# Last batch of the gate matrix written in four pieces on two queues and awaited in the next stage

## The chip, the cores and the metric

The kernel runs on one core of one Trainium2 chip, as one program of 48136 instructions. The metric is the device time of one execution in microseconds (us). A core has a matmul engine (TensorE, PE), a vector engine (VectorE, DVE), an activation engine (ScalarE, ACT), a general engine (GpSimd, POOL) and a synchronization engine (SyncE, SP). Transfers between the core's memory and main memory are issued from an engine's instruction stream and then run on 16 DMA engines which all queues share.

## The reference

Two transformer blocks on 512 tokens of width 1024. The part around the change is the product-key expert layer (PEER) of the first block: each token scores 128 + 128 sub-keys for each of 8 heads, keeps 16 of the pairs, and sums the outputs of these experts out of 128 x 128.

```python
def peer_ffn(x, w_query, sub_keys_1, sub_keys_2, w_down, w_up):
    ...
    top_s, pos = lax.top_k(cand, PEER_TOPK)
    expert_idx = jnp.take_along_axis(cand_idx, pos, axis=-1)
    gate = jax.nn.softmax(top_s, axis=-1).astype(x.dtype)
    ...
        u = w_down[ib]
        act = jax.nn.gelu(jnp.einsum("td,thkd->thk", xb, u), approximate=False) * gb
        v = w_up[ib]
        return jnp.einsum("thk,thkd->td", act, v)
```

Its result is added to the residual; a norm, the second block (attention, gating, 32 routed experts) and the last norm follow.

## The kernel before, in words

The program is a row of stages. Each is a `Stage` with its own buffers and semaphores, and `Stage.__exit__` clears the semaphores and puts a barrier over all engines (line 66), so a stage starts when every engine has finished the one before.

PEER isn't computed by gathering for the main 384 tokens (TD): it is computed densely. `stage_gate_matrix` (lines 1379 to 1551) turns the chosen experts and their weights into a full matrix of gates: for each token, 128 x 128 numbers that are zero but for the chosen pairs. It goes through the tokens in BATCHES = 6 batches of TB = 64. PE multiplies one-hot rows (line 1444), ACT copies the products out of PSUM into `out` (line 1488), a double buffer of 2 x 32 KB on each of 128 partitions, and SP writes each finished batch to the tensor `peer_gates` in main memory (line 1545, 4096 KB, one row of 32 KB for each partition; in a row, 128 keys by 64 tokens). Batch 5, the last, lies in the second half of `out`.

In the gaps, PE also computes the hidden values of experts in advance (line 1455); ACT bends them into `stash` (line 1466) and SP saves them as `peer_early` (line 1528, 192 KB each). SP also loads ahead what the next stage needs first: the first tiles of `wd`, `wu` and `hid`. SP's last waits (lines 1549 to 1551) are for the writes of the gates, the writes of the stash and these loads.

`stage_peer_experts` (lines 1554 to 1842) then runs STEPS = 64 steps over key rows, two rows in each step. A step has 24 matmuls of 384 columns (`late`, lines 1646 to 1648: hidden values of one key row) and 36 of 512 columns (`up`, lines 1655 to 1657: outputs of two key rows, accumulated in `Y` over the whole stage). Each float32 operand is split in a high part (ACT) and a low part (DVE). DVE multiplies the hidden values by the gates `gt` (lines 1753 and 1759), which SP reads back with `load_gt` (line 1588): 768 KB for two steps, four keys of all six batches, in runs of 1 KB. The 128 tokens left over (the first 128) are done by gather on POOL (`gather`, lines 1627 and 1630: 1 MB for each of 128 pairs, rows of 8 KB) and two DVE instructions for each pair (lines 1781 and 1793). The order of work at the start, by engine:

- SP: `load_gt(0, 0)`, two tiles of `wd` (line 1611), `load_gt(1, 1)`, and then `ahead` for each step: `wd`, `hid`, `wu` and, at every second step, `gt`, each behind the wait for the buffer that it overwrites.
- POOL: up to four gathers, then one for each that DVE has used up.
- ACT: `split_wd` of the first tile, `split_wu`, then `split_hid`, which waits for DVE's first multiplication by `gt`, then `split_wd` of the second tile.
- DVE: `low_wd`, then `weigh`, which waits for `gt`, and so on.
- PE: `late(0, 0)` after the first `low_wd`; `late(1, 1)` after the second.

Of the kernel before, what the change touches and what calls it, by code (L numbers as in the profile page):

```python
# [11 lines left out]
U32 = mybir.dt.uint32  # L12
# [1366 lines left out]
def stage_gate_matrix(nc, c, a):  # L1379
# [6 lines left out]
    with Stage(nc, "gates") as s:  # L1386
# [18 lines left out]
        wd_d = a["peer_wdT"]  # L1405
        wu_d = a["peer_pairs"]
        with s.block() as block:

# [52 lines left out]
            def _(act):  # L1461
# [40 lines left out]
                for b in range(BATCHES):  # L1502
# [9 lines left out]
                    if b < BATCHES - 1:  # L1512
                        with act.Fori(1, per) as q:
                            take(b, q)
                    else:
                        for q in range(1, per):
                            take(b, q, R * (per - q))
                early(2 * BATCHES - 2)
                early(2 * BATCHES - 1)

            @block.sync
            def _(sp):
# [13 lines left out]
                for b in range(BATCHES):  # L1536
# [7 lines left out]
                    sp.wait_ge(taken, R * per * (b + 1) + R)  # L1544
                    sp.dma_start(c.gates[b], out[:, b % 2, :, :].rearrange("p i t -> p (i t)")).then_inc(saved[b % 2], 16)
                save(2 * BATCHES - 2)
                save(2 * BATCHES - 1)
                for b in range(2):
                    sp.wait_ge(saved[b], 16 * (BATCHES // 2))
                    sp.wait_ge(stashed[b], 16 * BATCHES)  # L1550
# [3 lines left out]
def stage_peer_experts(nc, c, a):  # L1554
# [5 lines left out]
    with Stage(nc, "experts") as s:  # L1560
        wd = c.hT[:].rearrange("p k t -> p (k t)").rearrange("p (j n) -> p j n", j=4)
        wu, hid = c.wu, c.hid
        wd_hi, wd_lo = (s.sb(f"wd_{n}", [P, 2, D], F32R) for n in ("hi", "lo"))
        wu_hi, wu_lo = (s.sb(f"wu_{n}", [P, 2, 2, D], F32R) for n in ("hi", "lo"))
        hid_hi, hid_lo = (s.sb(f"hid_{n}", [P, 2, TD], F32R) for n in ("hi", "lo"))
        new = s.sb("new", [P, 2, TD])
        new_hi, new_lo = (s.sb(f"new_{n}", [P, 2, TD], F32R) for n in ("hi", "lo"))
        gt = s.sb("gt", [P, 2, BATCHES, 4 * TB])
        pair = s.sb("pair", [P, 4, 2 * D])
        slot = s.sb("slot", [P, 2 * U], U32)  # L1570
        dot = s.sb("dot", [P, 2, 2])
        bent = s.sb("bent", [P, 2, 2])
        part = s.sb("part", [P, 2, 2])
        Y = s.ps("Y", [P, 6, 512])
        H = s.ps("H", [P, 2, 512])
        wd_in, hid_in, paired = ([s.sem(f"{n}{i}") for i in range(4)] for n in ("wd_in", "hid_in", "paired"))
        wu_in, gt_in = ([s.sem(f"{n}{i}") for i in range(2)] for n in ("wu_in", "gt_in"))
        (wd_h, wd_l, wu_h, wu_l, hid_h, hid_l, new_h, new_l, h_done, gelued, gated, weighed, y_done, slotted, dotted,
         pair_bent, parted, added, paced, chain) = (s.sem(n) for n in (
# [3 lines left out]
        with s.block() as block:  # L1583

            @block.sync
            def _(sp):
# [17 lines left out]
                for i in range(4):  # L1604
                    if i < 2:
                        sp.sem_inc(wd_in[i], 16)
                        sp.sem_inc(wu_in[i], 16)
                    sp.sem_inc(hid_in[i], 16)
                load_gt(0, 0)
                for i in range(2, 4):  # L1610
                    sp.dma_start(wd[:, i, :], wd_d[STEPS + i]).then_inc(wd_in[i], 16)
                load_gt(1, 1)
                with sp.Fori(0, STEPS // U - 1) as r:
                    for u in range(U):
# [5 lines left out]
            def _(pool):  # L1620
                pool.sem_inc(added, 4)

                def gather(it, r, u, e):
# [1303 lines left out]
class Common:  # L2927
# [18 lines left out]
    def peer(self, ctx):  # L2946
# [3 lines left out]
        self.pair_gate = self.sb(ctx, "pair_gate", [P, PAIRS])  # L2950
        self.early = self.nc.dram_tensor("peer_early", [STEPS, P, TD], F32, kind="Internal").ap()
        self.gates = self.nc.dram_tensor("peer_gates", [BATCHES, NK, NK * TB], F32, kind="Internal").ap()

# [104 lines left out]
```

## Time and profile before

| | |
|---|---|
| median of 3 runs | 3527.06 us (3523.44 to 3539.63) |
| the profiled execution | 3532.37 us, its span 3530.6 us |
| PE busy in the span | 3202.8 us, 91% |
| DVE, ACT, POOL busy | 76%, 51%, 22% |
| gate stage, first to last matmul | about 939 to 1099 us |
| dense expert stage | about 1112 to 1910 us |

Times in the trace are microseconds from the span's start. The page names each instruction by its line and by output and inputs; SPq is SP's instruction stream, in which the transfers are issued. In the table by stretches, the column PEclk is the TensorE clock that was granted, as a share of full speed, and the DMA share is the mean busy share of the 16 DMA engines (it can pass 1, as the records of transfers overlap).

### The profile page before, as it was taken

To read this page: it belongs to the slowest core of one execution; us is meant where nothing else is said; L and a number is where in the kernel's file an instruction comes from. 1 tells how busy PE (TensorE), PEld (TensorE's weight loads), DVE (VectorE), ACT (ScalarE), POOL (GpSimd) and SP (SyncE) were. 2 spreads that over 40 slices of the span, in tenths; PEclk is the share of its full clock that TensorE was granted. 3 is DMA by queue.
4 is the path that set the end of the run, shared out by engine and by line. 5 is a ranking of instruction groups with operands and counts; after the bars stand their busy time and mean duration, and the time that the engine had idled before them with its cause. 6 is when DMAs were issued, how large, how long until landed. Compare 5 with 4: busy or idle time off the path is not lost. (4 is left out here: it accounts for less than half of the span.)

```text
span 3530.6 us, 48136 instructions
## 1 busy us (share of the span) xinstructions
PE 3202.8 (91%) x16519; PEld 2754.8 (78%) x16519; DVE 2697.6 (76%) x3822; ACT 1807.9 (51%) x2168; POOL 762.8 (22%) x478
## 2 busy tenths in 40 slices
PE   5999777999887999999997966599999999999996
PEld 5997666999887888888886845377788888878883
DVE  5786554696496878788887354599999999999994
ACT  3343342333585333333333241377777777777783
POOL 0000001445221444454542000211111111111110
PEclk8899788999999999999998976699999999999997
DMA  4220031334456999999985111699999999999993
GB/s 128 60 78 25 1 120 66 109 124 164 152 236 255 341 351 337 348 347 346 357 327 190 73 55 40 229 346 351 352 353 363 351 359 360 363 362 359 370 354 149
DMA packets 196091, 852.19 MB, mean 241 GB/s; under 512 B 22274, under 2 KB 104978, under 8 KB 152276
## 3 DMA queue, kind: packets, MB, share of 16 engines
q1 hardware_dynamic: 167492, 699.66, 54.0%
q0 software_dynamic: 28496, 151.16, 10.6%
q8 instruction: 65, 1.06, 0.1%
q14 instruction: 38, 0.31, 0.0%
HBM read 809.19 MB, written 59.38 MB: 246 GB/s over the span
## 5 line engine op out<-in xcount | busy, mean ns | idle before, releaser
L2704 DVE TENSOR_TENSOR moe_w_lo<-all_raw,moe_w_hi 128x2048 fp32r<-128x2048 f32 x298 | 676.0, 2286 | 68.8 <-ACT moe_w_hi L2644 66.4
L2644 ACT ACTIVATE moe_w_hi<-all_raw 128x2048 fp32r<-128x2048 f32 x298 | 567.0, 1915 | 84.8 <-PE moe_GU L2610 70.6
L2610 PE MATMUL moe_GU<-moe_w_hi,moe_x_lo 128*128 128x512 f32 x1056 | 418.6, 396 | 0.0
L2609 PE MATMUL moe_GU<-moe_w_lo,moe_x_hi 128*128 128x512 f32 x1056 | 418.1, 396 | 0.0
L2608 PE MATMUL moe_GU<-moe_w_hi,moe_x_hi 128*128 128x512 f32 x1056 | 418.1, 396 | 0.0
L1153 POOL TENSOR_TENSOR score_w_lo<-all_hT,score_w_hi 128x1024 fp32r<-128x1024 f32 x68 | 167.7, 2466 | 706.8 <-ACT score_w_hi L1218 706.8
L1781 DVE SCALAR_TENSOR_TENSOR experts_pair<-experts_pair,all_x_first 128x1024 f32<-128x1024 f32 x128 | 156.5, 1223 | 130.8 <-DMA experts_pair<-in_peer_pairs,experts_slot 130.8
L1630 POOL DMA_INDIRECT experts_pair<-in_peer_pairs,experts_slot x128 | 223.5, 1746 | 114.7 <-POOL experts_slot L1627 110.1
L2609 PEld LDWEIGHTS moe_GU<-moe_w_lo,moe_x_hi 128*128 128x128 f32 x1056 | 198.9, 188 | 48.8
L2610 PEld LDWEIGHTS moe_GU<-moe_w_hi,moe_x_lo 128*128 128x128 f32 x1056 | 198.9, 188 | 47.8
L2608 PEld LDWEIGHTS moe_GU<-moe_w_hi,moe_x_hi 128*128 128x128 f32 x1056 | 199.2, 189 | 46.3
L2704 DVE TENSOR_TENSOR moe_w_lo<-all_hT,moe_w_hi 128x2048 fp32r<-128x2048 f32 x98 | 223.0, 2284 | 2.4 <-ACT moe_w_hi L2644 1.4
L1627 POOL COPY experts_slot<-all_pair_id 128x1 uint32 x128 | 151.4, 1183 | 322.3 <-DVE all_h L1793 293.0
L2618 PE MATMUL moe_Y<-moe_w_hi,moe_hid_hi 128*128 128x512 f32 x528 | 215.2, 408 | 0.7 <-DVE moe_hid_lo L2734 0.7
L2619 PE MATMUL moe_Y<-moe_w_lo,moe_hid_hi 128*128 128x512 f32 x528 | 209.2, 396 | 0.0
L2620 PE MATMUL moe_Y<-moe_w_hi,moe_hid_lo 128*128 128x512 f32 x528 | 209.1, 396 | 0.0
L2644 ACT ACTIVATE moe_w_hi<-all_hT 128x2048 fp32r<-128x2048 f32 x98 | 187.5, 1914 | 38.6 <-PE moe_GU L2610 23.2
L2552 POOL DMA_INDIRECT pair_rows<-moe_y,moe_slot x33 | 48.1, 1457 | 728.2 <-ACT moe_y L2687 728.2
L1177 PE MATMUL score_H<-all_x_hi,score_w_hi 128*128 128x384 f32 (+1 forms) x544 | 190.3, 350 | 8.6 <-DVE all_x_lo L1291 8.6
L1178 PE MATMUL score_H<-all_x_lo,score_w_hi 128*128 128x384 f32 (+1 forms) x544 | 189.7, 349 | 0.0
L1179 PE MATMUL score_H<-all_x_hi,score_w_lo 128*128 128x384 f32 (+1 forms) x544 | 189.6, 349 | 0.0
L1646 PE MATMUL experts_H<-all_x_hi,experts_wd_hi 128*128 128x384 f32 x512 | 172.7, 337 | 16.2 <-DVE experts_wd_lo L1763 16.2
(473 smaller groups left out, 8170.3 us busy)
## 6 DMA issues: line engine op xcount, KB each, us to landing
all_raw<-in_w_moe SPq DMA_DIRECT2D x149, 2048.0 KB
all_hT<-in_w_moe SPq DMA_DIRECT2D x49, 2048.0 KB, 9.4
all_hT<-in_peer_wdT SPq DMA_DIRECT2D x128, 512.0 KB
all_wu<-in_peer_pairs SPq DMA_DIRECT2D x64, 1024.0 KB, 13.5
peer_gates<-gates_out SPq DMA_DIRECT2D x6, 4096.0 KB
experts_gt<-peer_gates SPq DMA_DIRECT2D x32, 768.0 KB, 9.7
all_hT<-in_w_in SPq DMA_DIRECT2D x40, 512.0 KB
out_w<-in_w_out SPq DMA_DIRECT2D x12, 1024.0 KB
```

The lines of the kernel that those rows point to most:

```text
L1177: pe.matmul(out, left, c.x_hi[:, k, at:T], start=(k == 0), stop=False)
L1178: pe.matmul(out, left, c.x_lo[:, k, at:T], start=False, stop=False)
L1179: mm = pe.matmul(out, low, c.x_hi[:, k, at:T], start=False, stop=(k == KD - 1))
L1630: pool.indirect_dma_start(out=pair[:, v, :], out_offset=None, in_=a["peer_pairs"][:, :], in_offset=bass.IndirectOffsetOnAxis(ap=slot[:, n: ...
L2608: pe.matmul(out, x_hi[:, kx, :], hi[:, k, :], start=False, stop=False)
L2609: pe.matmul(out, x_hi[:, kx, :], lo[:, k, :], start=False, stop=False)
L2610: mm = pe.matmul(out, x_lo[:, kx, :], hi[:, k, :], start=False, stop=(kx == KD - 1))
L2618: pe.matmul(Y[:, b, :], hid_hi[:, h, :], hi[:, f, cols], start=(h == 0), stop=False)
L2619: pe.matmul(Y[:, b, :], hid_hi[:, h, :], lo[:, f, cols], start=False, stop=False)
L2620: mm = pe.matmul(Y[:, b, :], hid_lo[:, h, :], hi[:, f, cols], start=False, stop=(h == KD - 1))
L2644: act.activation(w_hi[p % RING][:], piece_of(r, p), ACT.Copy).then_inc(w_high, 1)
L2704: dve.tensor_tensor(w_lo[p % RING][:], piece_of(r, p), w_hi[p % RING][:].bitcast(F32), ALU.subtract).then_inc(w_low, 1)
```

## The change

The last batch of gates is written not as one transfer of 4096 KB but as four of 1024 KB, by key: piece 0 holds keys 0 to 31 of each row, and so on (rows of 8 KB). SP issues piece 0; ACT issues pieces 1 to 3, behind its last copy out of PSUM and ahead of its last two stash activations. The pieces have two semaphores of their own (`c.tail`), which the gate stage doesn't wait for. It still waits for the other writes of the gates, for all writes of the stash, and for the loads ahead.

In the expert stage SP waits for piece 0 ahead of `load_gt(0, 0)`, and for the other three behind `load_gt(1, 1)`, ahead of the loop of `ahead`. POOL waits for those three ahead of its first gather. The gathers' buffer `pair` now lies where batch 5 lay in `out` (bytes 49152 to 81920 of each partition); `wu_hi`, `wu_lo`, `gt` and small buffers lie below it, with an unused filler `lead` and `hid_hi`, and the other buffers above. No instruction changes its shape.

```diff
+        def piece_in(i):
+            return out[:, (BATCHES - 1) % 2, i * NK // 4:(i + 1) * NK // 4, :].rearrange("p i t -> p (i t)")
+        def piece_out(i):
+            return c.gates[BATCHES - 1][:, i * (NK // 4) * TB:(i + 1) * (NK // 4) * TB]
...
+                act.wait_ge(taken, R * per * BATCHES + R)
+                for i in range(1, 4):
+                    act.dma_start(piece_out(i), piece_in(i)).then_inc(c.tail[1], 16)
                 early(2 * BATCHES - 2)
                 early(2 * BATCHES - 1)
...
-                    sp.dma_start(c.gates[b], out[:, b % 2, :, :].rearrange("p i t -> p (i t)")).then_inc(saved[b % 2], 16)
+                    if b + 1 < BATCHES:
+                        sp.dma_start(c.gates[b], out[:, b % 2, :, :].rearrange("p i t -> p (i t)")).then_inc(saved[b % 2], 16)
+                    else:
+                        sp.dma_start(piece_out(0), piece_in(0)).then_inc(c.tail[0], 16)
                 save(2 * BATCHES - 2)
                 save(2 * BATCHES - 1)
                 for b in range(2):
-                    sp.wait_ge(saved[b], 16 * (BATCHES // 2))
+                    sp.wait_ge(saved[b], 16 * ((BATCHES - b) // 2))
                     sp.wait_ge(stashed[b], 16 * BATCHES)
...
-        wd_hi, wd_lo = (s.sb(f"wd_{n}", [P, 2, D], F32R) for n in ("hi", "lo"))
         wu_hi, wu_lo = (s.sb(f"wu_{n}", [P, 2, 2, D], F32R) for n in ("hi", "lo"))
-        hid_hi, hid_lo = (s.sb(f"hid_{n}", [P, 2, TD], F32R) for n in ("hi", "lo"))
-        new = s.sb("new", [P, 2, TD])
-        new_hi, new_lo = (s.sb(f"new_{n}", [P, 2, TD], F32R) for n in ("hi", "lo"))
         gt = s.sb("gt", [P, 2, BATCHES, 4 * TB])
-        pair = s.sb("pair", [P, 4, 2 * D])
-        slot = s.sb("slot", [P, 2 * U], U32)
         dot = s.sb("dot", [P, 2, 2])
         bent = s.sb("bent", [P, 2, 2])
         part = s.sb("part", [P, 2, 2])
+        slot = s.sb("slot", [P, 2 * U], U32)
+        lead = s.sb("lead", [P, D - 28 - 2 * TD])
+        hid_hi = s.sb("hid_hi", [P, 2, TD], F32R)
+        pair = s.sb("pair", [P, 4, 2 * D])
+        wd_hi, wd_lo = (s.sb(f"wd_{n}", [P, 2, D], F32R) for n in ("hi", "lo"))
+        hid_lo = s.sb("hid_lo", [P, 2, TD], F32R)
+        new = s.sb("new", [P, 2, TD])
+        new_hi, new_lo = (s.sb(f"new_{n}", [P, 2, TD], F32R) for n in ("hi", "lo"))
...
+        s.sems += c.tail
...
+                sp.wait_ge(c.tail[0], 16)
                 load_gt(0, 0)
                 for i in range(2, 4):
                     sp.dma_start(wd[:, i, :], wd_d[STEPS + i]).then_inc(wd_in[i], 16)
                 load_gt(1, 1)
+                sp.wait_ge(c.tail[1], 48)
...
                 pool.sem_inc(added, 4)
+                pool.wait_ge(c.tail[1], 48)
...
+        self.tail = [self.nc.alloc_semaphore(f"gate_tail{i}") for i in range(2)]
```

## Rows read from the trace of the kernel before

**Rows 1.** Busy time by stretch; columns stand in the view's own second line.

```profile
core 0: us, PE busy (x) PEld busy (x) DVE busy (x) ACT busy (x) POOL busy (x), PEclk, DMA share, GB/s
1101.00:1104.00 3.00, 0.00 (x0) 0.00 (x0) 0.00 (x0) 0.00 (x0) 0.00 (x0) 0.60 1.21 513
1104.00:1105.00 1.00, 0.00 (x0) 0.00 (x0) 0.00 (x0) 0.00 (x0) 0.00 (x0) 0.50 0.08 33
1105.00:1109.00 4.00, 0.00 (x0) 0.00 (x0) 0.00 (x0) 0.00 (x0) 0.00 (x0) 0.50 1.22 524
1109.00:1110.00 1.00, 0.00 (x0) 0.00 (x0) 0.00 (x0) 0.00 (x0) 0.00 (x0) 0.50 0.04 12
1110.00:1112.00 2.00, 0.00 (x0) 0.00 (x0) 0.00 (x0) 0.00 (x0) 0.00 (x0) 0.50 0.53 191
1112.00:1114.00 2.00, 0.00 (x0) 0.00 (x0) 0.34 (x1) 1.43 (x2) 0.18 (x1) 0.50 0.00 0
1116.00:1126.00 10.00, 9.41 (x47) 9.09 (x47) 7.13 (x10) 5.41 (x8) 4.97 (x6) 0.87 1.03 408
1150.00:1880.00 730.00, 730.00 (x3538) 644.73 (x3537) 599.20 (x830) 269.48 (x416) 353.59 (x237) 1.00 0.92 343
```

**Rows 2.** Timeline at the border of the stages: start, duration, engine, line [idle before].

```profile
1098.71 0.60 ACT L1488 ACTIVATE gates_out<-gates_ps 128x512 f32<-128x512 f32 x1 [0.99 <-PE gates_ps L1444]
1099.03 0.34 PE L1455 MATMUL gates_H<-all_x_hi,gates_wd_lo 128*128 128x384 f32 x1
1099.20 0.87 ACT L1466 ACTIVATE gates_stash<-gates_H 128x384 f32<-128x384 f32 x2
1099.33 0.33 SPq L1545 DMA_DIRECT2D peer_gates<-gates_out  x1
1099.71 1.37 SPq L1528 DMA_DIRECT2D peer_early<-gates_stash  x2
1112.57 1.06 ACT L1689 ACTIVATE experts_wd_hi<-all_hT 128x1024 fp32r<-128x1024 f32 x1 [12.51 <-SPq L1606]
...
1113.03 0.39 SPq L1588 DMA_DIRECT2D experts_gt<-peer_gates  x1
...
1114.22 1.73 POOL L1630 DMA_INDIRECT experts_pair<-in_peer_pairs,experts_slot  x1 [1.05 <-issue]
```

**Rows 3.** SP's waits around the border: us in total, times, longest.

```profile
SPq L1550 <- DMA peer_early<-gates_stash: 10.4, 1, 10.4
```

**Rows 4.** The stash's and first gates' transfers by line.

```profile
L1528 SPq DMA_DIRECT2D peer_early<-gates_stash x12: 332/343/904, 970.5 to 1100.2; - x12
...
DMA to landing us min/median/max: 5.4/6.1/11.3
```

**Rows 5.** Timeline of the expert stage's first steps on DVE.

```profile
1118.28 0.56 DVE L1753 TENSOR_TENSOR all_hid<-all_hid,experts_gt 128x384 f32<-128x384 f32 x1 [3.40 <-DMA experts_gt<-peer_gates]
...
1120.38 1.23 DVE L1763 TENSOR_TENSOR experts_wd_lo<-all_hT,experts_wd_hi 128x1024 fp32r<-128x1024 f32 x1
...
1129.12 1.22 DVE L1781 SCALAR_TENSOR_TENSOR experts_pair<-experts_pair,all_x_first 128x1024 f32<-128x1024 f32 x1
...
1134.27 0.56 DVE L1753 TENSOR_TENSOR all_hid<-all_hid,experts_gt 128x384 f32<-128x384 f32 x1 [2.31 <-DMA experts_gt<-peer_gates]
...
1142.54 1.22 DVE L1763 TENSOR_TENSOR experts_wd_lo<-all_hT,experts_wd_hi 128x1024 fp32r<-128x1024 f32 x1
```

**Rows 6.** Timeline of the expert stage's first steps on PE.

```profile
1114.94 0.69 PE L1646 MATMUL experts_H<-all_x_hi,experts_wd_hi 128*128 128x384 f32 x1 [15.57 <-DVE experts_wd_lo L1763]
...
1121.66 0.44 PE L1646 MATMUL experts_H<-all_x_hi,experts_wd_hi 128*128 128x384 f32 x1 [0.59 <-DVE experts_wd_lo L1763]
...
1146.53 0.33 PE L1646 MATMUL experts_H<-all_x_hi,experts_wd_hi 128*128 128x384 f32 x1
```

**Rows 7.** The loads of `gt`: landing after issue.

```profile
DMA to landing us min/median/max: 8.5/9.7/19.7
```

**Rows 8.** Durations in the expert stage by tile: ns min/median/max.

```profile
L1767 DVE TENSOR_TENSOR experts_wu_lo<-all_wu,experts_wu_hi x128: 1214/1221/1236, 1118.8 to 1891.1; 128x1024 fp32r<-128x1024 f32 x128
```

## The prediction

> **What bounds the kernel now.** I read the busy time by stretch first, to see which engine is never idle beside the change. From 1150 to 1880 us, nearly the whole dense expert stage, PE is busy for 730 of 730 us at the full granted clock, and the DMA engines for 0.92 of it [rows 1]. So the stage goes by PE: when it starts earlier by some time, it ends earlier by that time, as long as transfers keep up. Nothing that the change moves inside this stretch can win anything, and DMA has only 8% of air there.
>
> Then I read the timeline at the border of the two stages. The last matmul of the gate stage starts at 1099.03 and the first of the expert stage at 1114.94, with 15.57 us idle [rows 2, 6]. That gap is all that the change can reach: 15.6 us are 0.44% of the run, and no version of this edit can save more there.
>
> What fills the gap is seen in SP's waits and in the stretches. SP issues the 4096 KB write at 1099.33 and the two last stash writes up to about 1101.1 [rows 2]. It then waits 10.4 us at line 1550, the wait for the **stash**, and not at line 1549 for the gates [rows 3]: the small transfers stand behind the large one in the same queue and land last, at about 1111.5. The bytes are seen to flow from 1100 to 1104, from 1105 to 1109 and from 1110 to 1111 or so: 4.19 + 0.39 = 4.58 MB in 11.1 us, 413 GB/s with the two holes counted [rows 1]. After 1111.5 come barrier and start: ACT begins at 1112.57, `load_gt(0, 0)` is issued at 1113.03 [rows 2]. From about 1111 to 1114 the DMA engines move nothing [rows 1].
>
> Last, the start of the expert stage on DVE and PE. The first matmuls need no gates. DVE then waits 3.40 us for `gt`, which is there at 1118.28, 5.25 us after its issue [rows 2, 5]; behind that stands the low part of the second `wd` (1120.38 + 1.23 = 1121.6), and PE's second group starts with it at 1121.66 after 0.59 us idle [rows 5, 6]. So the landing of the first `gt` is on the path too: what delays it delays PE one for one. From there on PE isn't idle.
>
> **The change part by part.**
>
> Removed from the path: the wait for the large write. But the wait that SP was seen in, for the stash, stays in the gate stage. The question is when the two stash writes land now. They are issued from SP's queue behind 1 MB instead of 4 MB, while 3 MB go through ACT's queue on the same engines.
>
> Issue times: ACT's last copy ends at 1099.31 [rows 2]. Three issues come now ahead of its two stash activations. ACT issues no transfer in this trace, so their price is bounded by SP's 0.33 us and by POOL's indirect 1.73 us each [rows 2]: 1.0 to 5.2 us. I take 1.0, since these are plain transfers like SP's. The activations (0.87 us for the pair) then end at about 1101.2, and the last stash is issued at 1101.5 instead of before 1101.1. The shortest landing of such a write is 5.4 us [rows 4]: not before 1106.9.
>
> Flow: 1.44 MB go through SP's queue. If both queues get the same bytes, they are through when 2.88 MB have moved, 7.0 us at 413 GB/s, at 1107.0, and landed with the 0.4 us that the last bytes took before (1111.1 to 1111.5) at **1107.4**. If the queues take turns row by row, each DMA engine has 8 + 8 + 8 rows of SP (8 KB, then twice 1.5 KB) against 24 rows of 8 KB of ACT, and both end together, at **1111.5** as before. No two queues from SP and ACT are seen together in this trace, so I take the middle, rounded to 1109.0, and keep both ends. The border moves by 2.5 us (bounds 4.1 and 0).
>
> The Trainium skill, DMA: Bandwidth & Descriptors, section on queues, rings and completion order, says that a DMA engine alternates between queues by whole packets of some 9 to 17 descriptors. By that, an estimate from that page, the SP queue would get a share of turns near that of its transfers: 1 MB, stash, stash, each against about 1 MB of ACT's, so the last stash would be through with two or three of the three pieces, at 1108.5 to 1111. The same page's rules for kernel authors speak against any gain from the second queue as such: spreading transfers over issuing engines brings no bandwidth. The traces so far have nothing that contradicts either.
>
> Start of the next stage: SP's wait for piece 0 costs nothing, as that piece is ahead of the stash in its queue. `load_gt(0, 0)` is issued at 1113.0 - 2.5 = 1110.5; its bytes began to flow about 1 us after issue before (issue 1113.03, none moved until 1114 [rows 1, 2]), so at 1111.5, when the last piece is through (all bytes need the same 11.1 us from 1100). Delay of `gt`: 0; at the good bound (issue at 1108.9, flow from 1109.9) up to 1.2 us of shared flow.
>
> SP's wait for pieces 1 to 3 stands ahead of the loop of `ahead`, behind both `load_gt`. Queued behind it are the loads of `wd`, `hid` and `wu` for later steps. It is over at about 1111.5, before SP would get there (1110.5 + 2). POOL's wait holds back all gathers until about 1111.5, where they would start at 1114.2 - 2.5 = 1111.7: nothing. If it lasted 2 us longer, the first use of a gathered pair at 1129.12 covers it, and the next use of DVE waits for `gt` anyway, 2.31 us before 1134.27 [rows 5].
>
> What is late next: after the first steps DMA works off a backlog (408 GB/s from 1116 to 1126 [rows 1]). The tightest place is the low part of `wd` that DVE ends at 1143.8, with PE taking it at 1146.53: 2.8 us of slack [rows 5, 6]. Transfers too start 2.5 us earlier, as they move out of the dead time from 1111 to 1114, so this stays uncovered by a hair but holds.
>
> The other order of buffers: same instructions, same shapes. DVE's `wu_lo` runs over four places and all 128 lie between 1214 and 1236 ns [rows 8], so address has cost nothing so far: 0. Two more semaphores to clear, two waits, more instructions: 0.
>
> **Sum.** -2.5 (border) + 0 (gt) + 0 (all else) = -2.5 us, against the profiled execution's 3532.37 us: 3529.9. That execution is 5.3 us above the median of the runs; from the median, 3527.06 - 2.5 = **3524.6 us**.
>
> **The rivals.**
>
> A, the stash stays last (no gain, so the change does not do what it says). By the row-by-row turns above, or because ACT's three issues cost nearer 1.73 us each (stash issued at 1105.7, landed at 1111.1 or later), or because the barrier's drain on ACT waits for transfers still under way; in this trace all had landed by the time of the barrier, so it can't tell. Against it: the short landing of 5.4 us for a stash write with little ahead of it [rows 4]. Also here: rows of 8 KB may flow slower than those of 32 KB; at the stage's 343 GB/s [rows 1] 4.58 MB take 13.4 us, 2.3 us more. Time: 3526 to 3529.5, say 3527.
>
> B, slower: the first `gt` starves. It is read in runs of 1 KB and may now share the engines with rows of 8 KB of the pieces. The slowest load of `gt` landed 19.7 us after issue [rows 7], which fits the second one, issued at the stage's start beside the gathers and waited for until 1134.27 [rows 5]; the first took 5.25. If the first were held as long, PE would lose 14.5 us against at most 4.1 won: 3537.5. It decides from a delay above what the border gains (2.5 to 4.1 us). Against it: by then at most 0.6 MB of the pieces are left, 1.5 us of flow.
>
> C, the full 4.1 us, with at most 0.3 us lost to the shared flow: 3523.0.
>
> D, the new places in memory or the shifted code change the pace of a stage. One per cent of the expert stage's 790 us would be 7.9 us, either way: 3519 or 3535. Only the narrow spread of [rows 8] speaks to it, and against it.
>
> **How the numbers follow.** Forecast with its surroundings (-1 to -3.5 us) 0.42; A 0.30; C 0.13; B 0.08; D 0.07, half each way. The range: from D's good side to the middle of B and D's bad side, widened because a median of three runs of this kernel itself lies within 12 us of its highest run: 3516 to 3535. The likeliest case alone: 3522 to 3528. A change of 0.5% is 17.6 us, about what a measurement of this kernel can tell from no change; the whole gap is 15.6 us, so faster by that much needs D or a fluke, and slower needs B at its worst with D on top. Faster 0.03, within 0.94, slower 0.03.
>
> **What the profile of the changed kernel would show.** SP's wait at the end of the gate stage still ends with a stash write, near 1109 (forecast), 1111.5 (A) or 1107.4 (C) if the last copy of ACT ends at 1099.3. Three issues on ACT's queue of about 0.35 us each. The first matmul of the expert stage 2.5 us earlier after ACT's last copy than the 15.6 us of before; the first multiplication by `gt` 5 to 6 us after its load's issue (B: more than 8). The stretch from 1150 to 1880 with the same matmul count and PE never idle; any other count is D. I am wrong if the gap shrinks by more than 4.1 us, which needs a stash write that lands faster than any did before, or if PE is idle after its second group.

## The result and the profile after

| | before | changed |
|---|---|---|
| median, the two run in turns | 3529.86 us (8 runs) | 3542.93 us (8 runs, 3535.12 to 3550.39) |
| ratio | | 1.0037, 95% interval 1.0023 to 1.0052 |
| the profiled execution, its span | 3532.37, 3530.6 us | 3535.12, 3533.3 us |

The change makes the kernel slower by some 13 us. That is above the whole range of the forecast (3516 to 3535) and has the other sign than its likeliest case. The profiled execution is the fastest of the eight, so it shows only a part of the loss: its span is 2.7 us longer, though by the rows below the border and the expert stage together take 11.4 us more. The parts ahead of and behind them happened to be 8.7 us shorter in it.

**The border** did what rival A says. The changed kernel's timeline answers to [rows 2] (start, duration, engine, line, what ended the idle time before it):

```profile
1096.29 0.60 ACT L1495 ACTIVATE gates_out<-gates_ps 128x512 f32<-128x512 f32 x1 [0.99 <-PE gates_ps L1451]
1096.92 2.05 ACTq L1527 DMA_DIRECT2D peer_gates<-gates_out  x3
1099.07 0.87 ACT L1473 ACTIVATE gates_stash<-gates_H 128x384 f32<-128x384 f32 x2 [2.18 <-issue]
1110.52 1.06 ACT L1708 ACTIVATE experts_wd_hi<-all_hT 128x1024 fp32r<-128x1024 f32 x1 [10.58 <-SPq L1622]
...
1096.91 0.33 SPq L1558 DMA_DIRECT2D peer_gates<-gates_out  x1
1099.59 1.57 SPq L1538 DMA_DIRECT2D peer_early<-gates_stash  x2
1110.98 0.39 SPq L1604 DMA_DIRECT2D experts_gt<-peer_gates  x1
```

The three issues take ACT 2.05 us, and they aren't alike (count: duration in ns as min/median/max):

```profile
L1527 ACTq DMA_DIRECT2D peer_gates<-gates_out x3: 401/445/1142, 1096.9 to 1097.8; - x3
```

Two take 0.40 and 0.45 us, not far from SP's 0.33 for a lone one, and the third 1.14. From the end of ACT's last copy (1096.89) to the issue of the first `gt` pass 14.09 us; before they were 1113.03 - 1099.31 = 13.72 [rows 2]. The border has moved by 0.37 us the wrong way. SP's waits there (line, what ended them, us in total, times, longest) answer to [rows 3]:

```profile
SPq L1563 <- DMA peer_early<-gates_stash: 8.3, 1, 8.3
SPq L1538 <- ACT gates_stash L1473: 2.3, 1, 2.3
```

The wait at the end is shorter by 2.1 us only because SP comes to it later: it waits 2.3 us for ACT's stash activations first (0.4 before). It still ends with a stash write, at about 1109.5 (ACT starts 1.06 us later, as it did before). Busy time by stretch in the changed kernel (columns: us, PE, PEld, DVE, ACT and POOL busy with their counts, clock, DMA share, GB/s):

```profile
1099.00:1103.00 4.00, 0.00 (x0) 0.00 (x0) 0.00 (x0) 0.87 (x2) 0.00 (x0) 0.59 1.04 426
1103.00:1105.00 2.00, 0.00 (x0) 0.00 (x0) 0.00 (x0) 0.00 (x0) 0.00 (x0) 0.50 1.00 412
1105.00:1108.00 3.00, 0.00 (x0) 0.00 (x0) 0.00 (x0) 0.00 (x0) 0.00 (x0) 0.50 1.01 406
1108.00:1109.00 1.00, 0.00 (x0) 0.00 (x0) 0.00 (x0) 0.00 (x0) 0.00 (x0) 0.50 0.81 317
1109.00:1111.00 2.00, 0.00 (x0) 0.00 (x0) 0.00 (x0) 0.48 (x1) 0.04 (x1) 0.50 0.00 0
1150.00:1880.00 730.00, 730.00 (x3488) 635.58 (x3488) 601.30 (x820) 268.36 (x409) 251.12 (x236) 1.00 0.92 341
```

The bytes flow without a hole up to just before 1109, when the stash is through too: both queues end together, and 1109 to 1111 stay empty as 1111 to 1114 did before [rows 1]. How they share the engines shows in the packets of each queue (q1 is SP's, q10 ACT's: packets, MB, share of 16 engines), here from 1099.9 to 1100.2, from 1100.2 to 1100.5 and from 1100.5 to 1100.8 us:

```profile
q1 hardware_dynamic: 16, 0.13, 109.6%
q10 hardware_dynamic: 16, 0.13, 103.0%
q1 hardware_dynamic: 16, 0.13, 103.7%
```

Sixteen rows of 8 KB from one queue, as many as there are DMA engines, then sixteen from the other: the queues take turns row by row. From 1104 to 1108, with SP's queue at the stash's rows of 1.5 KB, the counts stay alike and the bytes don't:

```profile
q10 hardware_dynamic: 183, 1.37, 83.3%
q1 hardware_dynamic: 189, 0.27, 17.8%
```

**The expert stage** is where the time went. PE is still busy for 730 of 730 us at full clock, but it gets through 3488 matmuls, not 3538 [rows 1]. The rows of one output buffer show why (line, operands, count: duration in ns as min/median/max, first and last start in us, form). First two of the kernel before:

```profile
L1655 PE MATMUL experts_Y<-experts_wu_hi,experts_hid_hi x384: 387/389/390, 1125.9 to 1905.5; 128*128 128x512 f32 x192
L1655 PE MATMUL experts_Y<-experts_wu_hi,experts_new_hi x384: 389/389/389, 1130.1 to 1909.6; 128*128 128x512 f32 x192
```

and the same two of the changed one:

```profile
L1674 PE MATMUL experts_Y<-experts_wu_hi,experts_hid_hi x384: 392/396/399, 1123.8 to 1914.4; 128*128 128x512 f32 x192
L1674 PE MATMUL experts_Y<-experts_wu_hi,experts_new_hi x384: 392/396/399, 1128.0 to 1918.6; 128*128 128x512 f32 x192
```

The same instruction with the same shape takes 396 ns for 389, and from the first of these starts to the last are 790.6 us for 779.6: **+11.0 us**. This difference of two starts is "the stage" below.

A second execution of the changed kernel (3551.82 us, span 3550.0, above all eight of the table) has a stage of 795.5 us; experiments 3 and 16, with the same places of the buffers, have 795.6 and 795.5:

```profile
L1674 PE MATMUL experts_Y<-experts_wu_hi,experts_hid_hi x384: 389/394/398, 1127.3 to 1922.8; 128*128 128x512 f32 x192
1150.00:1880.00 730.00, 730.00 (x3467) 633.63 (x3466) 597.15 (x818) 269.16 (x409) 273.46 (x233) 1.00 0.92 341
```

Matmuls overlap, so what counts is the distance between starts. PE's timeline in the middle of the stage, before:

```profile
1499.62 0.39 PE L1655 MATMUL experts_Y<-experts_wu_hi,experts_hid_hi 128*128 128x512 f32 x1
...
1501.66 0.39 PE L1655 MATMUL experts_Y<-experts_wu_hi,experts_new_hi 128*128 128x512 f32 x1
```

and in this second execution of the changed kernel:

```profile
1499.61 0.39 PE L1675 MATMUL experts_Y<-experts_wu_lo,experts_new_hi 128*128 128x512 f32 x1
...
1501.71 0.39 PE L1675 MATMUL experts_Y<-experts_wu_lo,experts_new_hi 128*128 128x512 f32 x1
```

Nine matmuls in 2.04 and in 2.10 us: 226.7 and 233.3 ns each. Averaged over the starts from 1150 to 1880 us, the 512-column ones went from 227.8 to 233.3 ns (36 in each of 63 steps: 12.5 us; before, too, the whole stretch is a little slower than the nine shown) and the 384-column ones from 174.4 to 176.7 (24 in each: 3.5 us), together 16.0 us of the 15.9 seen. In the first execution of the changed kernel the 512-column ones start every 233.3 ns too, but the 384-column ones every 173.4, no slower than before; that is why its stage is shorter.

### The profile page after: what moved, and what is told of

The parts are those of the page before. It is cut to its first block and busy times, and to the rows that moved or that the text cites. A ratio compares the mean times of both kernels' runs of the same rounds, so it can differ in the third digit from the quotient of the medians.

```text
span 3533.3 us, 48143 instructions
## 1 busy us (share of the span) xinstructions
PE 3210.9 (91%) x16519; PEld 2753.6 (78%) x16519; DVE 2705.9 (77%) x3822; ACT 1811.4 (51%) x2168; POOL 649.5 (18%) x478
## 3 DMA queue, kind: packets, MB, share of 16 engines
q8 instruction: 65, 1.06, 0.1%
## 5 line engine op out<-in xcount | busy, mean ns | idle before, releaser
L1714 ACT ACTIVATE experts_wu_hi<-all_wu 128x1024 fp32r<-128x1024 f32 x128 | 135.5, 1059 | 214.0 <-PE experts_Y L1676 204.9
L1649 POOL DMA_INDIRECT experts_pair<-in_peer_pairs,experts_slot x128 | 180.7, 1412 | 114.6 <-POOL experts_slot L1646 110.0
L1786 DVE TENSOR_TENSOR experts_wu_lo<-all_wu,experts_wu_hi 128x1024 fp32r<-128x1024 f32 x128 | 156.7, 1224 | 57.4 <-ACT experts_wu_hi L1714 56.8
## 6 DMA issues: line engine op xcount, KB each, us to landing
peer_gates<-gates_out SPq DMA_DIRECT2D x5, 4096.0 KB, 11.6
```

The source lines that it names most:

```text
L1649: pool.indirect_dma_start(out=pair[:, v, :], out_offset=None, in_=a["peer_pairs"][:, :], in_offset=bass.IndirectOffsetOnAxis(ap=slot[:, n: ...
```

## The experiments

The theory after the first profile: it is not the border, the waits or the queues, but **where the buffers begin**. In the compiled programs, counted modulo 512 bytes of a partition, `wu`, `hid_hi`, `hid_lo`, `new_hi`, `new_lo`, `wd` and the activations `x_hi` (a buffer of the whole program) all begin at 128 before. After the change `wu` and `x_hi` still begin at 128, but `hid`, `new` and `wd` at 192: the three small buffers of 16 bytes take 32 each, and `hid_hi` behind `lead` starts at the next multiple of 32, which makes 64 bytes. So `pair` too begins 64 bytes behind the start of batch 5, not at it as the section on the change has it, and the last 64 bytes of `hid_hi` lie on its first. That does no harm: `hid_hi` is written behind DVE's first multiplication by `gt`, so behind SP's wait for piece 0. A float32 buffer may lie at either place; what may count is how the stationary operand of a matmul (`hid` or `new`) lies against its moving one (`wu`). The rival: the pieces, their queue or the waits disturb the stage.

**1. The new order, 64 bytes less filler.** All else of the change stays.

```diff
-        lead = s.sb("lead", [P, D - 28 - 2 * TD])
+        lead = s.sb("lead", [P, D - 44 - 2 * TD])
```

> The changed kernel's expert stage is longer: its 512-column matmuls (lines 1674 to 1676) show 396 ns each instead of 389, those of 384 columns 337 as before, and the first to the last 512-column matmul takes some 11 us longer. This run is the changed kernel with the filler `lead` shorter by 64 bytes, so that all buffers behind it (hid_hi, pair, wd, hid_lo, new, new_hi, new_lo) lie 64 bytes lower; order and transfers stay. Theory 1, the place of the stationary operand: in the kernel before, hid_hi, hid_lo, new_hi and new_lo start at multiples of 128 bytes, in the changed kernel 64 bytes past one; here they are back at multiples of 128. It expects 389 ns and 11 us less than the changed kernel, about 3532 us beside 3543, about equal to the kernel before. Theory 2, the region: wu_hi and wu_lo lie lower and the stationary operands are spread; 64 bytes change nothing: 396 ns and about 3543. Theory 3, a mere shift of code or the second queue: 396 ns as well.

3532.59 us (11 runs), ratio to the kernel before 1.0004 (0.9995 to 1.0013): the loss is gone. Its row:

```profile
L1674 PE MATMUL experts_Y<-experts_wu_hi,experts_hid_hi x384: 387/389/390, 1128.1 to 1909.3; 128*128 128x512 f32 x192
```

The stage takes 781.2 us, 1.6 more than before. The new order, `pair` where batch 5 lay, the pieces and the waits cost nothing that can be told from no change.

**2. The kernel before, its buffers from `hid_hi` on 64 bytes up.**

```diff
         wu_hi, wu_lo = ...
+        shift = s.sb("shift", [P, 16])
         hid_hi, hid_lo = ...
```

> The kernel before with 64 bytes of filler ahead of hid_hi, so that hid_hi, hid_lo, new, new_hi, new_lo, gt, pair and the small buffers lie 64 bytes higher; wd, wu and all else stay. Theory 1 (place of the stationary operand): 396 ns for each 512-column matmul of the expert stage and +11 us, about 3541 beside 3530. Theory 2 (region or order): 389 ns, no change. Theory 3 (code, second queue): no change.

3540.51 us, ratio 1.0028 (1.0014 to 1.0042). An unused buffer of 64 bytes slows the kernel before by some 10 us; the stage takes 791.9 us:

```profile
L1656 PE MATMUL experts_Y<-experts_wu_hi,experts_hid_hi x384: 394/394/394, 1124.4 to 1916.3; 128*128 128x512 f32 x192
```

**3. The new order alone**, in the kernel before: one write of 4096 KB, no new waits, the buffers declared as in the diff ahead.

> The kernel before with the changed kernel's order of buffers (lead included) and nothing else of the change: one transfer, all waits in the gate stage. Theories 1 and 2 (place or region): 396 ns for each 512-column matmul and +11 us, as the whole change. Theory 3 (the second queue, the pieces, the awaited semaphores): 389 ns and no change.

3541.01 us, ratio 1.0036 (1.0023 to 1.0049), stage 795.6 us: the change's whole loss without its pieces.

```profile
L1657 PE MATMUL experts_Y<-experts_wu_hi,experts_hid_hi x384: 389/394/398, 1126.1 to 1921.7; 128*128 128x512 f32 x192
```

**4. The pieces alone**, with the old order; since `pair` then lies elsewhere, SP waits for all pieces at the end of the gate stage.

```diff
+                sp.wait_ge(c.tail[0], 16)
+                sp.wait_ge(c.tail[1], 48)
```

> The changed kernel with the order of buffers of before, and SP's waits for the four pieces moved to the end of the gate stage (they can't stand later, since gt would be loaded over what is being written). It has the pieces, the second queue and ACT's three issues. Theories 1 and 2: 389 ns, the expert stage as before; the border is that of before or up to 1.5 us later, as ACT's issues (2.05 us for three in the changed kernel) push the stash writes back: 3530 to 3532. Theory 3: 396 ns and +11 us.

3532.63 us, ratio 1.0007 (0.9996 to 1.0019), stage 1906.5 - 1126.9 = 779.6 us as before. SP's wait still ends with a stash write:

```profile
SPq L1564 <- DMA peer_early<-gates_stash: 8.3, 1, 8.3
```

None of its waits for the pieces has a row. Moving them into the next stage wins nothing, because when the stash has landed they have too.

**5. Which distance counts: the routed experts.** In that later stage `x_hi` of the gathered tokens begins at 160 modulo 512. 96 bytes ahead of it bring it to 256.

```diff
+        shift = s.sb("shift", [P, 24])
```

> The kernel before with 96 bytes of filler in the routed experts' stage ("moe") ahead of x_hi: x_hi, x_lo, hid_hi and hid_lo there, the stationary operands, start 32 bytes past a multiple of 128 in the kernel before, and at a multiple of 128 here. Its 512-column matmuls (lines 2608 to 2610, 2618 to 2620) show 396 ns on average, as the misplaced ones of the expert stage do. Theory 1 (place of the stationary operand, in any stage): 389 ns instead of 396, and up to 4750 matmuls x 6.7 ns = 32 us less, if that stage goes by PE: 3498 to 3510. Rival (those 396 ns have another cause, or 64 bytes matter and 32 don't): 396 ns, 3530. Rival (the stage is held by its transfers at 350 to 364 GB/s): 389 ns, but PE waits in their place, 3515 to 3530.

3531.17 us, ratio 1.0001 (0.9987 to 1.0014). The stage's costliest matmuls went from a mean of 396 to 395 ns (median 395 or 396 to 393). Their moving operands, the weights, begin at 128, so a distance of 128 bytes is about as slow as one of 32, and "begin at a multiple of 256" is no rule.

**6 and 7. One operand at a time, first try.** 64 bytes before and 64 after `hid` (6) or `wu` (7), so that what follows lies 128 up.

> The kernel before with 64 bytes of filler ahead of hid_hi and hid_lo and 64 bytes behind them, so that hid_hi and hid_lo start 64 bytes past a multiple of 128, and new, new_hi, new_lo, gt and pair at multiples of 128 again. Theory 1 in its narrow form (each matmul goes by the place of its own stationary operand): 394 to 396 ns for matmuls with hid_hi and hid_lo, 389 for those with new_hi and new_lo in the same step, and half of the 11 us: 3535. Rival (something of the whole stage, as the place of gt, pair or the small buffers): all alike, 394 to 396 and +11 us, or all 389 and no change.

> The kernel before with 64 bytes of filler ahead of wu_hi and 64 bytes behind wu_lo: only these two, the moving operands of the 512-column matmuls, start 64 bytes past a multiple of 128; the stationary operands are at multiples of 128. Theory 1 (stationary operand alone): 389 ns, no change, 3530. Rival (any operand of a matmul): 394 to 396 ns and +11 us, 3541.

3541.45 us, 1.003 (1.0019 to 1.0042), and 3541.4 us, 1.0037 (1.0025 to 1.0049). All 512-column matmuls of the stage were slow in both (393 or 394 ns by the median), as `new` (6) and the distance from `wu` to `hid` and `new` (7, again 64) had moved too. They don't separate the operands; in 6 `hid` is 64 and `new` 128 bytes further than `wu`, and both cost about the same.

**9. `hid` alone.** 64 bytes ahead, 448 behind, so that `new` is back at 128.

```diff
+        shift = s.sb("shift", [P, 16])
         hid_hi, hid_lo = ...
+        back = s.sb("back", [P, 112])
```

> The two runs before showed that the fillers of e6 and e7 didn't isolate what they meant to: their sum of 128 bytes left new_hi and new_lo at another place within 512 bytes. In all kernels with 389 ns the stationary operands of the 512-column matmuls start 128 bytes past a multiple of 512 (a tile of 128 columns of float32 is 512 bytes); in all with 394 to 396 ns they don't. This run is e6 with the second filler 448 bytes: hid_hi and hid_lo 64 bytes up, new_hi, new_lo, gt, pair and the small buffers 512 up. Theory 1b (each matmul goes by the place of its own stationary tile within 512 bytes): matmuls with hid_hi and hid_lo 394 to 396 ns, those with new_hi and new_lo 389, and 5 to 6 us more: 3536. Rival (a matter of the whole stage or of the program): all alike, 3541 or 3530.

3536.4 us, ratio 1.0016 (1.0001 to 1.003), stage 786.8 us, and in one and the same step:

```profile
L1657 PE MATMUL experts_Y<-experts_wu_hi,experts_hid_hi x384: 393/394/398, 1125.9 to 1912.7; 128*128 128x512 f32 x192
L1657 PE MATMUL experts_Y<-experts_wu_hi,experts_new_hi x384: 389/389/398, 1130.1 to 1916.8; 128*128 128x512 f32 x192
```

Only the moved stationary operand's matmuls are slow, with `wu`, the transfers and the neighbours the same. That settles that it is a matter of the single matmul and its operands, and not of the whole stage.

**11. `wu` alone**, in the same manner (64 ahead, 448 behind), so that the distance is 64 bytes the other way.

> e7 with the second filler 448 bytes: of the matmuls' operands only wu_hi and wu_lo, the moving ones, lie 64 bytes up, all others are at their place within 512 bytes. Theory 1b, stationary operand alone: 389 ns, 3530. Rival (moving operand as well, or stationary and moving against each other): 394 to 396 ns, 3541.

3532.8 us, ratio 1.0004 (0.9988 to 1.002), stage 782.6 us. This side costs only 3.0 us, and by operand:

```profile
L1657 PE MATMUL experts_Y<-experts_wu_hi,experts_hid_hi x384: 387/392/392, 1126.4 to 1909.0; 128*128 128x512 f32 x192
L1658 PE MATMUL experts_Y<-experts_wu_lo,experts_hid_hi x384: 394/394/397, 1126.6 to 1909.2; 128*128 128x512 f32 x192
L1659 PE MATMUL experts_Y<-experts_wu_hi,experts_hid_lo x384: 388/388/397, 1126.9 to 1909.4; 128*128 128x512 f32 x192
```

**12. All 64 up.** The 64 bytes stand ahead of all buffers of the stage.

> The kernel before with 64 bytes of filler ahead of all buffers of the dense expert stage, so that moving and stationary operands of the 512-column matmuls keep their places against each other and all lie 64 bytes off. Theory 1b (the place as such): 394 to 396 ns, 3541. Rival (only the place of one against the other counts): 389 ns, 3530; then the 384-column matmuls, whose moving operand x_hi doesn't move, are the ones that grow, by up to 3 ns in 337.

3535.49 us, ratio 1.0003 (0.999 to 1.0015), stage 780.4 us. The median lies 5.5 us above that of the kernel before in the same round, which the ratio over the rounds doesn't bear out.

```profile
L1656 PE MATMUL experts_Y<-experts_wu_hi,experts_hid_hi x384: 389/389/397, 1127.1 to 1907.5; 128*128 128x512 f32 x192
L1647 PE MATMUL experts_H<-all_x_hi,experts_wd_hi x512: 335/338/689, 1115.9 to 1895.4; 128*128 128x384 f32 x171
```

At 192 and 192 the 512-column matmuls are as fast as at 128 and 128: the **relative** place counts. The 384-column ones, whose `x_hi` does not move with them, are slower (338 for 334).

The experiments so far together; the distance is that of `hid` and of `new` from `wu`, modulo 512 bytes, and the durations are medians:

| kernel | `hid`, `new` from `wu` | 512-column matmuls with `hid`; `new` | stage |
|---|---|---|---|
| before | 0, 0 | 389; 389 ns | 779.6 us |
| changed, its two executions | +64, +64 | 396; 396 and 394; 394 | 790.6 and 795.5 |
| 2 | +64, +64 | 394; 394 | 791.9 |
| 6 | +64, +128 | 394; 393 to 394 | 790.6 |
| 7 | +64, +64 | 394; 394 | 791.5 |
| 9 | +64, 0 | 394; 389 | 786.8 |
| 11 | -64, -64 | 388 to 394 by operand | 782.6 |
| 12 | 0, 0 (at 192) | 389; 389 | 780.4 |

**14. `wd` alone**, 64 ahead and 448 behind, one execution.

> The kernel before with 64 bytes of filler ahead of wd_hi and 448 bytes behind wd_lo: only these, the stationary operands of the 384-column matmuls, lie 64 bytes off against their moving operand x_hi; the 512-column matmuls keep theirs. e3 and e12, which have wd so too, showed 338 to 340 ns for the 384-column matmuls, the changed kernel 335 although its wd lies at the same place. If it is the place: 338 to 340 ns for the 384-column matmuls, 389 for the others, and 4 to 5 us more. If it is something else of those two programs: 335 to 337 as in the kernel before.

3527.53 us. The 384-column matmuls show 336 ns, but the stage takes 778.8 us: no loss.

```profile
L1648 PE MATMUL experts_H<-all_x_hi,experts_wd_hi x512: 333/336/687, 1115.6 to 1893.1; 128*128 128x384 f32 x171
```

**15 and 16. The changed kernel and experiment 3 once more**, one execution each, since the first profile has the 384-column matmuls near their old pace.

> The changed kernel once more, for a second profile. If its 384-column matmuls (335 ns on average beside 338 to 340 in e3, with all buffers at the same places) are a property of the program: 335 ns again. If it differs from execution to execution: another value.

> e3 (the kernel before with the changed kernel's order of buffers) once more, for a second profile. A property of the program: 338 to 340 ns for the 384-column matmuls again. If it differs from execution to execution: another value, 335 perhaps.

3551.82 and 3543.49 us, both with a stage of 795.5 us. The 384-column row of the changed kernel, first in the first profile, then in the second:

```profile
L1665 PE MATMUL experts_H<-all_x_hi,experts_wd_hi x512: 333/335/688, 1112.9 to 1902.0; 128*128 128x384 f32 x171
```

```profile
L1665 PE MATMUL experts_H<-all_x_hi,experts_wd_hi x512: 333/338/689, 1116.4 to 1910.4; 128*128 128x384 f32 x171
```

The same program has them at 335 in one execution and at 338 in another, and the stage at 790.6 and 795.5; the 512-column ones stay at 394 to 396.

**8. The stash first**, on top of experiment 1: ACT does its last two stash activations ahead of its three issues, SP saves the stash ahead of piece 0, and POOL waits for piece 0 too. This takes away the cause of rival A.

```diff
+                early(2 * BATCHES - 2)
+                early(2 * BATCHES - 1)
                 for i in range(1, 4):
                     act.dma_start(piece_out(i), piece_in(i)).then_inc(c.tail[1], 16)
-                early(2 * BATCHES - 2)
-                early(2 * BATCHES - 1)
...
+                        save(2 * BATCHES - 2)
+                        save(2 * BATCHES - 1)
                         sp.dma_start(piece_out(0), piece_in(0)).then_inc(c.tail[0], 16)
...
+                pool.wait_ge(c.tail[0], 16)
```

> The changed kernel with lead 64 bytes shorter (e1) and another order of issues at the border: ACT makes its two stash activations ahead of its three transfers, and SP issues the two stash writes ahead of piece 0; POOL waits for piece 0 too. The border theory: in the changed kernel the stash writes land last, since they are issued 2.2 us later and share the engines with 4 MB, so the gate stage ends no earlier; here they have little ahead of them and land about 5.4 us after their issue. The gate stage then ends 5 to 6 us earlier after ACT's last copy, the first load of gt ends 3 to 5 us earlier, and the time is 3 to 5 us below e1, about 3527. Rival (gt is then held back by the pieces, which land as late as ever): the first multiplication by gt starts as late after ACT's last copy as in e1, 3532.

3531.21 us (12 runs), ratio 0.9997 (0.9987 to 1.0007). SP's waits and its timeline:

```profile
SPq L1563 <- DMA peer_early<-gates_stash: 6.0, 1, 6.0
SPq L1604 <- DMA peer_gates<-gates_out: 2.9, 1, 2.9
```

```profile
1101.82 0.83 SPq L1538 DMA_DIRECT2D peer_early<-gates_stash  x2
1102.69 1.19 SPq L1560 DMA_DIRECT2D peer_gates<-gates_out  x1
1114.31 0.39 SPq L1604 DMA_DIRECT2D experts_gt<-peer_gates  x1
...
1119.38 0.56 DVE L1773 TENSOR_TENSOR all_hid<-all_hid,experts_gt 128x384 f32<-128x384 f32 x1 [6.06 <-DMA experts_gt<-peer_gates]
```

PE's first matmul comes 11.97 us after its last, for 15.94 in the changed kernel and 15.57 before: 4.0 and 3.6 us won at the border. But now the first `gt` waits 2.9 us for piece 0, a new wait in place of the old one. DVE's first multiplication starts 18.03 us after ACT's last copy ended (1101.35); in the changed kernel it was 1116.12 - 1096.89 = 19.23, and before 18.97 [rows 2, 5]. So 1.2 us are left against the one and 0.9 against the other, and they can't be seen in the time.

**10 and 13. The routed experts at 128.** 480 bytes ahead of that stage's `x_hi` bring it to 128, where the weights begin: in the kernel before (10), and with experiment 8 (13).

```diff
+        shift = s.sb("shift", [P, 120])
```

> The kernel before with 480 bytes of filler ahead of x_hi in the routed experts' stage: x_hi, x_lo, hid_hi, hid_lo there start 128 bytes past a multiple of 512, as the fast ones of the dense expert stage; with 96 bytes (e5) they started at a multiple of 256 and nothing changed. Theory 1b: 389 ns instead of 396, and up to 32 us less if the stage goes by PE: 3498 to 3512. Rival (held by transfers, or another cause of its 396 ns): 3530.

> e8 (the changed kernel with its operands at their places, stash writes first) and e10 (the routed experts' stationary operands at theirs) in one kernel. If the two gains are independent: 389 ns in both stages, the first multiplication by gt about 1 us earlier after ACT's last copy than in the kernel before, and 6 to 7 us below it: 3523 to 3525. Rival (e10's 5.6 us below the kernel before were chance, as its stage's waits ate what its matmuls gave): within 2 us of the kernel before, 3528 to 3532.

10: 3524.35 us, ratio 0.9983 (0.9969 to 0.9996). 13: 3530.44 us, ratio 0.9993 (0.9979 to 1.0007). The matmuls do get faster; the costliest groups (busy us, mean ns) of the kernel before and of 10:

```profile
L2610 PE MATMUL moe_GU<-moe_w_hi,moe_x_lo 128*128 128x512 f32 x1056 | 418.6, 396 | 0.0
```

```profile
L2611 PE MATMUL moe_GU<-moe_w_hi,moe_x_lo 128*128 128x512 f32 x1056 | 412.4, 390 | 0.0
```

But PE's waits in this stage grow; one row of the kernel before, two of 10:

```profile
PE moe_X L2574 <- DMA moe_xg<-h_rows,moe_slot: 39.7, 9, 31.8
```

```profile
PE moe_X L2575 <- DMA moe_xg<-h_rows,moe_slot: 47.4, 10, 31.4
PE moe_GU L2582 <- DVE moe_hid L2730: 5.5, 16, 0.4
```

Of the shorter matmuls, 13 us come back as waits for gathered tokens and for DVE, and from its first matmul to its last the stage takes 1215.5 us for 1218.0. In 13 PE waits 50.9 us for the gathered tokens, the stage takes 1218.1, and no gain is left. Where this stage is unchanged it took from 1210.6 us (experiment 7) to 1223.3 (15), so single profiles can't settle 5 us. The interval of 10 lies below 1, but 13 did not confirm it: a gain of 5 us is possible and not shown. No version here clearly beats the kernel before.

## Why the prediction was wrong

**What bounds the kernel: right.** PE bounds the expert stage, and the border was all the change's own mechanism could reach. The conclusion that nothing inside the stage could move held for the waits and transfers, not for PE's own pace.

**The sum.** Its terms were -2.5 us (border), 0 (`gt`) and 0 (all else). Measured they are +0.37, 0, and +11.0 in one execution and +15.9 in the other, all of it in the term that I had put at nothing for the order of buffers. The base was 2.8 us low as well: 3527.06 is the median of three runs, and over eight it is 3529.86 (the highest of the three lies 12.6 us above their median, not within 12).

**The border: the step to 1109.0 failed, rival A held.** I took the middle of two ways in which queues share the engines. The packets show the bad end of my range, turns row by row: both queues are through together, when all bytes are. Experiment 8 shows it once more: piece 0, 1 MB issued at 1102.69, lets the first `gt` go at 1114.31, 11.6 us later; at 413 GB/s alone it would need 2.5 us, an estimate from [rows 1]. I weighed there the Trainium skill's DMA: Bandwidth & Descriptors, section on queues, rings and completion order, with its turns by whole packets of some 9 to 17 descriptors, and took a turn for about a whole transfer, eight rows on each engine: 1108.5 to 1111, on the issue times forecast. Counted from the end of ACT's last copy that is 9.2 to 11.7 us, and the row has 1109.5 - 1096.9 = 12.6, against 12.2 before. A turn was one row here, so that reading of it was wrong; how many descriptors a row makes no row tells. A's 3527, no gain, was the right size for this part: experiment 4, ratio 1.0007.

**ACT's issues: mis-sized.** Forecast 1.0 us, measured 2.05, within the bounds of 1.0 to 5.2. I took SP's price for a lone transfer, 0.33 us, three times. Two of ACT's three cost 0.40 and 0.45, the third 1.14, and the trace of before had such a row: SP's last stash write, the third transfer in a row on its queue, is the 904 ns of "332/343/904" [rows 4]. The stash activations start 2.18 us after the end of ACT's last copy, where they had started 0.11 us ahead of it [rows 2]: 2.3 us later.

**The first `gt`: right, delay 0.** From its issue to DVE's first multiplication pass 5.14 us (1110.98 to 1116.12), before 5.25 by [rows 2, 5]. Rival B did not occur, and the waits for the pieces are in no row of the waits; that B's 3537.5 lies nearer to the result than any other figure is chance. C did not occur; experiment 8 came near its 4.1 us at the stage's start, with 3.6, and lost all but 0.9 of it to the wait for piece 0.

**"The other order of buffers: 0": the step that decided.** It rested on DVE's `wu_lo` at four places [rows 8]. DVE's rows indeed say nothing: 1212 to 1228 ns in the changed kernel too. But the engine that bounds the stage is PE, and for PE I had no row with operands at another distance; all of the stage's matmuls of before had their operands at 128. A row of DVE is no bound for PE. The trace of before even had a hint: the same form, 512 columns at full clock, stood at 389 ns in the expert stage and at 396 in the routed experts, whose `x_hi` begins at 160. Rival D named this case with 7.9 us and half of 0.07; its mechanism holds, with 11.0 and 15.9 us in the two executions. Experiment 3 without the pieces gives 1.0036, experiment 1 with all but 64 bytes gives 1.0004: all of the loss that can be measured is the placement.

**The other waits of the stage** changed much and for nothing: DVE's wait for gathered pairs fell from 130.8 to 30.8 us in total and ACT's wait for PE at `wu_hi` rose from 10.6 to 204.9, while PE, the bound, was slower (with the places put right in experiment 1, 123.4 and 7.1). Read alone, the first would have looked like a gain.

## What to carry to other kernels

When a change moves or reorders buffers, list where each operand of the bounding engine's instructions begins, before and after, and compare the durations of the same form on that engine, not on another; a filler of 64 bytes may be worth more than the change. Splitting a large write over two queues did not bring forward the small ones issued behind a part of it, for the queues share the engines row by row; ask which small transfer lands last, and what will wait instead once it doesn't. And where the pace differs from one execution of a kernel to the next, take more than one profile before you explain a few microseconds.

## What the runs showed of the hardware

- A matmul of 512 columns in float32 at full clock started every 226.7 ns in the nine shown (227.8 over the stage) when both operands begin at the same place modulo 512 bytes, and every 233.3 when the stationary one lies 64 bytes further (389 against 394 to 396 ns by duration). 128 bytes further were as slow (393 to 394 ns in experiment 6, 393 in 5), and so were 32 in the routed experts of the kernel before (395 to 396). 64 bytes the other way lay between, 388 to 394 ns by operand. The Trainium skill, SBUF — State Buffer, section Operand start alignment, says that a float32 operand may start at any multiple of four bytes, and that its measurements of this timed nothing; the rows here are about the time. The same page's section on who interferes with whom says that "PE and ACT never wait on anyone." These runs contradict no part of that, since one matmul's two operands are not two engines.
- Why it is so stays open. That the unit is 512 bytes is taken from the fillers of 64 + 448 bytes in experiments 9, 11 and 14; a distance of 256 bytes was in no run, so a period of 256 isn't ruled out.
- Matmuls of 384 columns differ between executions of one program (335 and 338 ns, 4.9 us of the stage). The slow pace was seen only with `wd` 64 bytes further than `x_hi`: in those six traces the row of `x_hi` and `wd_hi` has a median of 335 to 338 ns, and in all twelve others 334. But `wd`'s place alone does not bring it about each time (experiment 14, and the first profile of the changed kernel), and what else is needed stays open.
- The price of issuing a plain transfer differed more by its place in the row than by engine or size. On ACT's queue the three of 1 MB took 0.40, 0.45 and 1.14 us in the changed kernel; on SP's, one of 1 MB and two of 192 KB took 0.33, 0.43 and 0.90 before. The third was the slow one in every such row here, on either queue; why is not shown.
- Two queues with rows waiting took turns one row at a time on each DMA engine, with rows of 8 KB against rows of 8 KB and, by the counts, with 1.5 KB against 8 KB too.
